# Head norms four chunks at a time, scores fused with their maximum, copies moved to ScalarE and 16 modulation pages of layer 0 moved later, in a two-layer decoder step

## What is computed

```python
mod = silu(c) @ w_ada + b_ada                      # six parts: shift, scale, gate, twice
h = rms_norm(x, g_mix) * (1 + sc1) + sh1
q, k, v, u, g = split(h @ w_in)                    # 4 heads x 2 maps x 64 for q and k
q, k = rms_norm(q, q_gain), rms_norm(k, k_gain)    # over each 64 channels
s = where(rel >= 0, q @ k.T * 64 ** -0.5 + rel_bias, -inf)
p = softmax(s); a = p[map 0] - lam * p[map 1]; o = a @ v
o = rms_norm(o, subln) * (1 - lambda_init)         # over each head's 128 channels
merged = g0 * (o @ w_branch[:512]) + g1 * (pool(u) @ w_branch[512:])
x = x + gt1 * (merged @ w_out)
h2 = rms_norm(x, g_ffn) * (1 + sc2) + sh2
x = x + gt2 * (swiglu(h2) if layer == 0 else top2_of_8_experts(h2))
```

## Time and profile before

| | us |
|---|---|
| median of 3 runs | 1598.79 (1598.11 to 1599.88) |
| the profiled execution's own time | 1603.74 |
| its span | 1602.1 |
| PE busy | 1564.8 (98%) |
| DVE busy | 541.4 (34%) |
| ACT busy | 181.5 (11%) |

### The profile page before, as it was taken

One profiled execution on the slowest core, in us unless ns is written; L12 is line 12 of the kernel. 1 busy time (PEld: TensorE's weight loads), 2 busy tenths in 40 slices (PEclk: granted clock), 3 DMA queues, 4 the chain that ended last, 5 costly groups with the idle time before them and its releaser, 6 DMA issues.

```text
span 1602.1 us, 37184 instructions
## 1 busy us (share of the span) xinstructions
PE 1564.8 (98%) x16734; PEld 987.4 (62%) x16734; DVE 541.4 (34%) x1182; ACT 181.5 (11%) x486; POOL 69.5 (4%) x118
## 2 busy tenths in 40 slices
PE   7999999999999999999999999999999999999987
PEld 3777898999997878944444444444444445555554
DVE  4368378666554784741001101110111011101132
ACT  2102303111112032131000000000000000000000
POOL 1112400000000110010000000000000000000010
PEclk9999999999999999999999999999999999999999
DMA  9999969666359745579999999999999999999995
GB/s 362 362 387 365 285 220 322 231 224 215 128 176 317 241 160 181 171 277 377 416 410 388 418 419 402 417 416 403 418 404 416 418 401 418 414 405 417 407 377 181
DMA packets 174339, 535.30 MB, mean 334 GB/s; under 512 B 12535, under 2 KB 101413, under 8 KB 161378
## 3 DMA queue, kind: packets, MB, share of 16 engines
q1 hardware_dynamic: 158274, 494.58, 80.8%
q0 software_dynamic: 8768, 28.96, 5.3%
q10 hardware_dynamic: 7136, 9.34, 1.8%
HBM read 517.47 MB, written 15.82 MB: 333 GB/s over the span
## 4 chain that ended last, share of the span: by engine, by line
PE 86%; DMA 9%; DVE 3%; issue 1%; ACT 1%; SPq 1%; ACTq 0%; DVEq 0%
PE banks L1890 33%; PE banks L1911 16%; PE banks L1204 14%; PE banks L1565 13%; DMA ring<-in_w_exp_up 5%; DMA ring<-in_w_in 2%; PE banks L1475 2%; PE banks L1745 2%; PE banks L1236 1%; DVE inv L2510 1%; PE banks L1732 1%; PE banks L1583 1%; DMA ring<-in_w_ada 1%; DMA ring<-in_w_exp_down 0%; PE banks L1614 0%
## 5 line engine op out<-in xcount | busy, mean ns | idle before, releaser
L1890 PE MATMUL banks<-ring,xT 128*32 128x448 f32 x3072 | 301.4, 539 | 2.9 <-DMA ring<-in_w_exp_up 2.9
L1890 PE MATMUL banks<-ring,area 128*32 128x448 f32 x3072 | 301.7, 539 | 1.3 <-DMA ring<-in_w_exp_up 0.8
L1565 PE MATMUL banks<-hT,ring 128*128 128x264 f32 x1024 | 238.0, 387 | 5.2 <-ACT hT L898 3.7
L577 DVE TENSOR_TENSOR area<-banks,area 128x448 f32<-128x448 f32 x48 | 45.7, 953 | 573.5 <-ACT area L1162 573.5
L1911 PE MATMUL banks<-area 128*32 128x256 f32 x3840 | 226.8, 379 | 1.7 <-issue 1.6
L1565 PEld LDWEIGHTS banks<-hT,ring 128*128 128x128 f32 x1024 | 191.9, 190 | 40.5 <-issue 8.6
L1890 PEld LDWEIGHTS banks<-ring,xT 128*32 128x32 f32 x3072 | 108.1, 110 | 163.7 <-issue 152.0
L1890 PEld LDWEIGHTS banks<-ring,area 128*32 128x32 f32 x3072 | 104.8, 110 | 167.4 <-issue 159.1
L1911 PEld LDWEIGHTS banks<-area 128*32 128x32 f32 x3840 | 132.8, 110 | 106.7 <-issue 45.3
L1162 ACT ACTIVATE area<-banks 128x448 f32<-128x448 f32 x48 | 26.1, 543 | 776.7 <-PE banks L1890 776.7
L1911 PE MATMUL banks<-ring,area 128*32 128x256 f32 x1536 | 89.2, 379 | 1.8 <-DMA ring<-in_w_exp_down 1.2
(11 more groups left out here) (362 smaller groups left out, 1255.2 us busy)
## 6 DMA issues: line engine op xcount, KB each, us to landing
ring<-in_w_exp_gate SPq DMA_DIRECT2D x128, 896.0 KB, 15.1
ring<-in_w_exp_up SPq DMA_DIRECT2D x128, 896.0 KB, 17.1
area<-in_w_exp_down SPq DMA_DIRECT2D x62, 1024.0 KB, 16.2
ring<-in_w_ada SPq DMA_DIRECT2D x96, 512.0 KB, 8.5
ring<-in_w_in SPq DMA_DIRECT2D x32, 1024.0 KB, 12.6
ring<-in_w_exp_down SPq DMA_DIRECT2D x32, 1024.0 KB
area<-in_w_exp_down SPq DMA_DIRECT2D x31, 512.0 KB
ring<-in_w_ff_gate SPq DMA_DIRECT2D x11, 1024.0 KB, 7.3
```

Source lines behind the costliest of these rows:

```text
L577: dve.tensor_tensor(F["act_tok"][:, t, :].rearrange("p (i n) -> p n i", i=BODY), bank[3 + t][:, 0:SLICE].rearrange("p (n i) -> p n i", i=B ...
L1565: mm = pe.matmul(bank[b][:, 0:T], w[:, c, :], hT[:, c, :], start=(c == 0), stop=(c == DC - 1))
L1890: mm = pe.matmul(bank[t + 3 * half][32 * g:32 * g + 32, 0:SLICE], tokens[:, t, 32 * r:32 * r + 32], w[half][:, SLICE * g:SLICE * (g + 1)], ...
```

## The change

- **Head norms.** Four chunks are squared, and four matmuls with 32 columns of ones write their sums into the four 32-row strips of one bank (`sum_four_qk`, `sum_four_o`). One root and one reciprocal serve four chunks; a matmul of 32 rows by 128 columns (`spread_inv`) then spreads each row over a chunk's partitions, and DVE multiplies from PSUM. There are three groups in a layer (q, k, o).
- **Scores.** q's gain carries the factor 1/8, and one `tensor_tensor_reduce` for each map adds the bias, negates and takes the minimum. `score(n)` now waits for `top_ready`.
- **Copies.** The bias rows, the samples' queries and keys, v, and the new rows are copied by ACT in place of DVE.
- **Pages.** Of the 32 modulation pages in layer 0's input projection 16 remain: two behind each of the first four pairs, four behind the next two. Pages 32 to 39 go behind the branch products, pages 40 to 47 into the feed-forward, two behind each of four pairs that carry two already.
- **Order.** The first 16 chunks are made by pairs (`z_whole`). The transposes of the samples' queries stand behind chunk 11 in place of chunk 10, those of the keys behind gate chunk 16 in place of chunk 12. `past_scores(0)` begins behind the copy of chunk 15, and the samples' own scores follow the second one. In each layer DVE also makes four sums of h (L2549), which no product reads as long as `Z_HALVED` is empty.
- Code for a split form of the first 16 chunks is added under `Z_HALVED`, whose two tuples are empty; none of it runs.

```diff
+        LATER_ADA = (16, 18, 20, 22, 24, 28, 32)
+
         def later_ada(l, i):
 
-            return range(16 + 2 * (i - 1), min(16 + 2 * (i + 1), 48)) if l == 0 and i % 2 else range(0)
+            return range(LATER_ADA[i // 2], LATER_ADA[i // 2 + 1]) if l == 0 and i % 2 and i < 13 else range(0)
...
+        def last_ada(i):
+
+            return range(36 + 2 * i, 38 + 2 * i) if 2 <= i <= 5 else range(0)
 
...
                 for j in range(0, 8, 2):
+                    for n in range(32, 40) if (kind, l, j) == ("out", 0, 0) else ():
+                        yield ada_page(0, n)
                     for n in range(2) if (kind, l, j) == ("out", 0, 6) else ():
...
+                def root_four(g):
+                    act.wait_ge(s.sum_four, 3 * l + g + 1)
+                    if g:
+                        act.wait_ge(s.inv_four, 3 * l + g)
+                    act.activation(root[:, 0, :], bank[SUM_FOUR[g]][:, 0:T], ACT.Sqrt, bias=eps[:, 0:1],
+                                   scale=1.0 / (P if g == 2 else HD)).then_inc(s.root_four, 1)
+
+                def read_sample_rows(i):
+                    act.wait_ge(s.qs_mm, 2 * l + i + 1)
+                    act.copy(ATT[("qs_tok", "ks_tok")[i]], bank[(1, 7)[i]][0:NS, :]).then_inc(s.ks_ready, 1)
+
...
+                if l == 0:
+                    act.wait_ge(s.bias_mm, H + 1)
+                    act.copy(bias_s[:, :], bank[4][0:64, 0:PAST + 1]).then_inc(s.bias_out, 1)
+                    for h in (3, 0, 1, 2):
+                        act.copy(PRO["bias_row"][:, h, :], bank[BIAS_BANK[h]][:, 0:WL]).then_inc(s.bias_out, 1)
...
                     for m in range(2):
-                        act.activation(prob[:, m, :], prob[:, m, :], ACT.Exp, bias=top[:, m:m + 1], scale=1.0,
+                        act.activation(prob[:, m, :], prob[:, m, :], ACT.Exp, bias=top[:, m:m + 1], scale=-1.0,
                                        accum_out=total[:, m:m + 1]).then_inc(s.exp_out, 1)
...
+                def sum_four_qk(g):
+
+                    if l == 0:
+                        pe.wait_ge(s.bias_out, H + 1)
+                        pe.wait_ge(s.state_out, 2 * g)
+                    for q in range(4):
+                        pe.wait_ge(s.qk_square, 8 * l + 4 * g + q + 1)
+                        mm = pe.matmul(bank[SUM_FOUR[g]][32 * q:32 * q + 32, 0:T], halves[:, 48:80], sq[:, 4 * g + q, :],
+                                       start=True, stop=True, skip_group_check=True)
+                    mm.then_inc(s.sum_four, 1)
+
+                def spread_inv(b, q):
+
+                    pe.matmul(bank[b][:, 0:T], const("spread")[32 * q:32 * q + 32, :], inv[32 * q:32 * q + 32, :],
+                              start=True, stop=True).then_inc(s.spread_four, 1)
+
+                def spread_qk(j):
+
+                    if l == 0 and j == 0:
+                        pe.wait_ge(s.rest_in, 16 * 3)
+                    pe.wait_ge(s.inv_four, 3 * l + j // 4 + 1)
+                    for k in range(j, j + 2):
+                        if k >= 2:
+                            pe.wait_ge(s.qk_ready, 8 * l + k - 1)
+                        spread_inv(6 + k % 2, k % 4)
+
...
+                            z_ada(u - 1)
+                        z_whole(u)
+                        z_ada(u)
+                        if u in (6, 7):
+                            spread_qk(2 * u - 8)
+                    if l == 0 and u in STATE_AT:
+                        turn_state(STATE_AT.index(u))
+                    if u in (2, 4):
+                        sum_four_qk((u - 2) // 2)
+                    if u in (3, 4):
+                        spread_qk(2 * u - 6)
+                    if u == 5:
+                        turn_sample_queries()
...
+                def sum_four_o():
+
+                    pe.wait_ge(s.o_square, 4 * (l + 1))
+                    for h in range(H):
+                        mm = pe.matmul(bank[SUM_FOUR[2]][32 * h:32 * h + 32, 0:T], ones[:, 0:32], o_sq[:, h, :],
+                                       start=True, stop=True, skip_group_check=True)
+                    mm.then_inc(s.sum_four, 1)
 
                 pe.wait_ge(s.gate_out, GC * (l + 1))
                 pe.wait_ge(s.y_ready, 4 * (l + 1))
@@ -1734,8 +1942,12 @@
                     mm.then_inc(s.pb_mm, 1)
                     if j == 1:
                         pe.wait_ge(s.o_out, 4 * (l + 1))
-                    if 1 <= j < 5:
-                        sum_o(j - 1)
+                    if j == 2:
+                        sum_four_o()
+                    if j == 4:
+                        pe.wait_ge(s.inv_four, 3 * (l + 1))
+                        for h in range(H):
+                            spread_inv((0, 1, 6, 7)[h], h)
...
+                if l == 0:
+                    for n in range(32, 40):
+                        modulation(0, n, 7)
                 out_projection(l)
...
+            step(dve.tensor_scalar(vecT[:, 138:138 + LAYERS], vecT[:, 138:138 + LAYERS], SCALE, None, ALU.mult))
...
+                def z_read(i):
                     dve.wait_ge(s.pages_used, used_up("z", l, i))
-                    z, b = i % QC, bank[2 + i % 4]
-                    if i // QC != 2:
...
+                def inv_four(g):
+                    dve.wait_ge(s.root_four, 3 * l + g + 1)
+                    if g:
+                        dve.wait_ge(s.spread_four, 12 * l + 4 * g)
+                    dve.reciprocal(inv[:, :], root[:, 0, :]).then_inc(s.inv_four, 1)
...
-                    dve.wait_ge(s.score_out, 8 * l + n + 1)
-                    step(dve.tensor_reduce(top, prob, AX.X, ALU.max))
-                    dve.tensor_scalar(top, top, -1.0, None, ALU.mult).then_inc(s.top_ready, 1)
+                    for m in range(2):
+                        r = dve.tensor_tensor_reduce(out=prob[:, m, :], in0=bank[4 + 2 * (n % 2) + m][:, 0:w], in1=bias[:, h, S - w:S],
+                                                     scale=-1.0, scalar=3.0e38, op0=ALU.add, op1=ALU.min, accum_out=top[:, m:m + 1])
+                    r.then_inc(s.top_ready, 1)
...
+                        z_read(2 * u)
+                    if u == 3:
+                        inv_four(0)
+                    if u in (4, 5):
+                        norm_qk(2 * u - 8)
+                        norm_qk(2 * u - 7)
+                    if halved:
+                        z22(u)
+                    if l and u + 1 in Z_HALVED[l]:
+                        sum_z(u + 1, 0)
+                        sum_z(u + 1, 1)
+                    if u == 5:
+                        inv_four(1)
+                    if u in (6, 7):
+                        norm_qk(2 * u - 8)
+                        norm_qk(2 * u - 7)
+                    if l == 0 and u in STATE_AT:
+                        read_state(STATE_AT.index(u))
+                    if l == 0 and u == 2:
                         lam_sums()
-                    if 4 <= i < 12:
-                        norm_qk(i - 4)
...
-                        past_scores(i - 14)
+                    if u == 7:
+                        early_mod()
+                    if u == 6:
+                        last_inputs()
+                    if not halved:
...
+                past_scores(0)
+                past_scores(1)
...
-                if l == 0:
-                    read_mod(l, 1, 32, 47, spare).then_inc(s.mod_out, 1)
-                past_scores(2); read_v(0); past_scores(3); read_v(1); past_scores(4); past_scores(5); past_scores(6); read_new()
-                past_scores(7); scores(0); window_sums(); scores(1); weights(0); pooled_minus_own(0)
+                own_scores()
+                for b in range(2, NS):
+                    past_scores(b)
...
-                    if 2 <= j < 6:
-                        norm_o(j - 2)
+                    if j == 3:
+                        inv_four(2)
+                    if j >= 5:
+                        for h in ((0, 1), (2,), (3,))[j - 5]:
+                            norm_o(h)
```

537 lines of the change are left out of this document (335 added, 202 removed).

## The result

| | kernel before | changed kernel |
|---|---|---|
| median, first measurement | 1599.60 us (6 runs, 1598.11 to 1601.23) | 1607.53 us (6 runs, 1603.87 to 1609.29) |
| ratio, 95% interval | | 1.0046 (1.0036 to 1.0056) |
| median, second measurement | 1599.84 us (17 runs) | 1606.36 us (6 runs) |
| ratio, 95% interval | | 1.0036 (1.0024 to 1.0048) |
| profiled execution, its span | 1603.74, 1602.1 us | 1607.95, 1606.3 us |

The change makes the kernel slower: the two ratios average 1.0041, some 6.6 us (the medians lie 7.9 and 6.5 us apart). The forecast was +4.1. On the forecast's base of 1598.79 us the average ratio gives 1605.3, within the range given; the first median taken by itself, 1607.53, lies 0.5 us above the range's end of 1607.0.

What follows compares the result with a forecast made beforehand. PE's instruction list was taken as the bound (busy 1564.8 of 1602.1 us), so DVE's relief wins nothing. Terms -0.1 - 1.5 - 0.1 + 2.2 + 3.6 = +4.1 us on 1598.79 gave 1602.9 us, range 1599.0 to 1607.0.

Steps and rivals of the forecast that it cites:

- Step 1: Modulation pages on PE: regrouped batches -0.1 us, PE's waits for pages in the first 16 chunks gone, -1.5 us.
- rival A: Keys land in 4.1 us, score(2)'s wait vanishes: +0.5 us, 1599.3; decides below 5.1 us issue to landing; chance 0.25.
- Step 2: Norms of q and k on PE: sum-fours at 0.58 and spreading pairs at 0.65, 7.5 us against 7.6: -0.1 us.
- Rival C: Row groups run side by side: spreading pairs at 0.53 us, the o norm's four spreads at 0.6; 1600.9; chance 0.10.
- Step 3: O norm in the branch products: PE waits for DVE, 1.1 us later in each of two layers, +2.2 us.
- Step 4: DVE's list ahead of layer 0's scores: PE waits at score(2) for score 0's minimum, +3.6 us; layer 1, 0.
- At some 108.1: Time in us at which DVE would begin layer 0's past scores, behind chunk 15 and the last norms.
- Step 5: The rest: DVE's unread sums of h, ACT's bias copies and DVE's modulation readings hidden; nothing added to the sum.
- Rival B: Fused scores on DVE cost some 0.5 us more each, PE waits: some +9 us, 1608; chance 0.10.
- D: PE's list is not the bound; a lighter DVE wins more than the new waits cost: 1595; chance 0.05.

Runs made afterwards that it cites:

- five traces named above: Traces with fused scores, norms in groups of four, and DVE list and pages as in the changed kernel up to score(2) of layer 0.
- after_fill: Changed kernel plus four matmuls, never read, in PE's wait for layer 0's first hT chunk; 1.0034 of the kernel before.
- the fill: Four 128x264 matmuls, never read, in PE's wait for layer 0's first hT chunk; added to the kernel before, 1.0005 of it.
- the best: Changed kernel with the fill, scores 0 and 1 earlier on DVE, o norm one product earlier, old q and k norms; 0.9979 of the kernel before.
- best_no_fill: The best without its four unread matmuls in PE's first wait; 0.9980 of the kernel before.

## Why the prediction was right, and where it was not

**The sign and the kind** were right: a loss of a few us, from PE's new waits for DVE's list, in a kernel where DVE's relief is worth nothing (the forecast gave "slower by over 0.2%" no more than 0.52). Its size, +4.1, was short of 6.6, and it came that near partly by luck: the term for score(2) was 1.5 us too high, while the norms of q and k were 1.4 too low and the clock's 2.6 were missing. By its steps:

**Step 1, pages.** Right in its rows: a batch of eight takes 3.59 us (220.70 to 224.29; forecast 3.61), one of two 1.00, the 1.5 us of waits are gone, and PE never waits for pages of w_out. The pages themselves come out 0.3 us dearer and not 0.1 cheaper: behind the branch products, up to layer 1's first chunk, PE needs 7.50 us more (220.70 to 489.78 against 223.10 to 484.68), and 7.22 were taken out ahead. The rows of layer 1's first chunk stand at the end of this section. What the step left out, and rival A had half of: the keys land sooner with the pages gone, by anything from 0.1 to 1.8 us in the median, and putting them back made PE's wait at score(2) 1.1 us longer than the longest with fused scores and without them. But A's mark was wrong: it put the end of the wait at 5.1 us from issue to landing, and at 4.7 there were still 2.1 us of it.

**Step 2, norms of q and k: mis-sized in layer 1.** The failing sentence is "I take 0.65 at 264: 5.2 in all. The sum is 7.5 against 7.6". The 0.65 is right start to start (0.64 and 0.65), and so is 0.58 for the sum-four; but a price read between two starts leaves out that the steps on either side are 0.1 longer each. A pair costs 0.84 (three more pairs: 2.53 us), near the upper bound of 0.89, which I had given to matmuls one after the other. That is not what happens: the two matmuls of a pair start 7 ns apart, and four spreads take 0.66 (199.08 to 199.74), as long as two. In layer 1 the norms cost 1.2 us more than before, not 0 (from the first chunk to score(2) 91.26 against 90.08); undoing them gave that back (1.17). In layer 0 the same reading leaves 0.1 us for them: 103.13 to PE's coming at score(2) against 109.18, with 7.22 of pages, 1.5 of page waits and 2.6 of clock taken into account. There most groups stand behind a batch of pages, which has the longer steps at its sides already: a pair of chunks between two batches, with no norm near, takes 7.32 us (45.90 to 53.22), not 7.12. Why undoing the norms then gave 0.8 us in layer 0 stays open. Rival C had its four spreads right (0.66, it said 0.6) but not its pairs (0.64, it said 0.53), and failed as the sum went up. The rule of the Trainium skill ("TensorE: Matmul & The Clock Gate", "Why this matters for your kernels") puts the starts of matmuls in distinct row groups at most 4 ns apart; the trace agrees that they run side by side, but has them 7 ns apart.

**Step 3, the o norm.** Right in the total: 17.57 us against 17.6, in both layers, with waits of 0.46 and 0.92 (forecast 0.6 and 1.1). Within it the four spreads were put at 1.1 and took 0.66, and the steps at their sides and at the sums made up for it. The loss was not the method's: with the reciprocal one product earlier, and the multiplications behind product 4's, the same norm takes 15.95.

**Step 4, score(2) of layer 0: right in the mechanism, wrong in its parts.** Forecast 3.6, measured 2.1 and 1.3. PE came there at 138.14, not at 134.8: 2.6 of the 3.3 us were lost to the clock and 0.4 by a later start. "At some 108.1" was 3.4 us too early, because the copy of chunk 15 waits behind the norms, and these for PE's spreads. These two misses cancel, which is luck. What remains is the keys: the forecast's own list had 3.6 us of waits for them (12 tiles at 1.45 us from 116.5 would end at 133.9, it said 137.5), and they were 2.3 and 1.5. The wait followed them in all five traces named above. So it was the keys' landings, mis-sized, that made the wait, and not the lead that the step works out for PE: in after_fill PE comes 2.6 us earlier and waits no longer, as the past scores all stand behind chunk 15 now and DVE moves with PE. The keys' lateness hurts because score 0 stands at the end of the list; moving two scores ahead took the whole wait away, with 1.0 us of waits for keys still there. In layer 1 the forecast was 0 with a bound of 1.5, and PE came 0.2 us after score 0's minimum; other traces have up to 0.6.

**Step 5, the rest: the clock was missing.** Nothing in the trace before hinted at it: the same wait of 2.04 us had cost no clock there. It fell in that wait or right behind it in nine of the ten traces of changed kernels without the fill, and in none of three with it. It explains 2.6 us of the 6.9 between the two traces. How much of the 6.6 by the ratios it makes is less sure: the fill gained nothing measurable in the kernel before, 0.7 us or so in the changed one (inside the intervals) and nothing measurable in the best, and with one trace of the kernel before without it I can't say how often it falls there. The record's mean granted clock of every execution points to a part of it: 0.9964 on average over the 12 executions of the changed kernel, 0.9973 over 64 of the kernel before, 0.9974 over the 5 of after_fill. A difference of 0.0009 of 1600 us would be some 1.4 us; that is an estimate, it counts idle time too, and it doesn't say where the clock fell.

**The sum against the trace**, to the routing: clock +2.6, pages +0.3, page waits -1.5, norms of q and k +0.1 and +1.2, score(2) +2.1, o norm +2.1: +6.9, as found. Rival B (fused scores dear) was wrong by its sign: two fused passes of 128 columns take 0.42 us. D had no sign of itself.

PE's timeline at layer 1's first chunk, before and changed:

```profile
484.68 10.92 PE L1565 MATMUL banks<-hT,ring 128*128 128x264 f32 x48 [1.68 <-ACT hT L898]
...
489.78 21.60 PE L1784 MATMUL banks<-hT,ring 128*128 128x264 f32 x96 [1.68 <-ACT hT L950]
```

## What to carry to other kernels

A price for a small group of matmuls of another shape must be read across it, from the last matmul ahead to the second behind, or from a stage with and without it; start to start hides the handover. In a list written out by hand, a cheaper operation that waits for another engine is not cheaper for what is queued behind it: ask first what stands behind its wait. And when a change loses in three small places, mend each before giving it up: here two edits of DVE's order and the old norms of q and k turned +0.4% into -0.2% (best_no_fill).

## What the runs showed of the hardware

- Between matmuls of 128x128 weights and ones of 128x32 or 32x128 (f32, 264 columns) the issue step is 0.32 us, and the first step behind them 0.33, against 0.2225 within a chunk: 0.2 us for each excursion, whether it holds two or four matmuls.
- Matmuls of 32 rows in different row groups start 7 ns apart, four 128x32 strips likewise; a pass of such a group takes 0.32 us (rows) or 0.23 (strips), and an f32 group makes two, so that in f32 four spreads cost what two do.
- In or right behind a wait of 2.04 us the granted clock fell to half, and 1.5 to 2.6 us were lost, in nine of ten traces of changed kernels; in the tenth, with the same instructions around it, and in the kernel before it did not. Waits of 3.00 and 3.15 us were followed by it too, and one of 2.08 at score(2) was not. With work in the wait the clock stayed whole in three traces of three, but the 1.7 us could not be found again at the end of the program.
- DVE's fused add and minimum with an accumulator takes 0.21 us to the next issue for 128 columns and 0.35 for 256, its readout of 0.08 included; three steps for twice 128 took 0.97.
